# Mixer D of a hybrid encoder layer: heads computed in pairs, with scores on 64 rows of the array, the key bias added in the maximum's instruction, probabilities scaled before they are turned, and values as the stationary operand

## The reference

```python
c = jnp.cumsum(jax.nn.log_sigmoid(f_logit.astype(F32)), axis=1).transpose(0, 2, 1)
for blk in range(seq // D_QBLOCK):            # 8 blocks of 128 queries
    s = jnp.einsum('bhqd,bhkd->bhqk', qh[:, :, q0:q1], kh[:, :, :q1]) * HEAD_DIM ** -0.5
    s = s + c[:, :, q0:q1, None] - c[:, :, None, :q1]
    causal = jnp.arange(q1)[None, :] <= (q0 + jnp.arange(D_QBLOCK))[:, None]
    p = jax.nn.softmax(jnp.where(causal, s, -jnp.inf), axis=-1)
    outs.append(jnp.einsum('bhqk,bhkd->bhqd', p, vh[:, :, :q1]))
```

## Time and profile before

| | us |
|---|---|
| median of 3 runs | 2148.26 (2148.06 to 2148.79) |
| the profiled execution, its own time | 2147.65 |
| its span, first to last instruction | 2145.9 |
| first to last filler matmul of mixer D | 615.25 to 964.0 |
| TensorE idle in 615.25 to 964.50 | 0.57 |

### The profile page before, as it was taken

How to read it: one execution, slowest core, us unless ns; L and a number is a source line. 1 busy time by engine, 2 the same in 40 slices (tenths; PEclk the granted TensorE clock), 3 DMA queues, 4 the chain that set the end, 5 groups by cost and what they waited for, 6 DMA issues and landing times. The chain is left out here.

```text
span 2145.9 us, 23081 instructions
## 1 busy us (share of the span) xinstructions
PE 2065.3 (96%) x7129; PEld 1091.9 (51%) x7130; DVE 1073.3 (50%) x2957; ACT 430.1 (20%) x929; POOL 686.9 (32%) x605
## 2 busy tenths in 40 slices
PE   7999999999999999999999999899999999999992
PEld 5445887574644555554444554444444444444440
DVE  6121455549452222221224756786666666666645
ACT  2111332334321111112221222011111111111113
POOL 1752002212132221202442001355544555544531
PEclk9999999999999999999999999999999999999996
DMA  5421000011112121216336004699999999999984
GB/s 142 120 89 39 21 15 26 20 45 64 50 65 74 68 74 49 69 49 235 103 93 226 30 40 162 248 335 345 354 357 352 358 356 358 352 355 346 345 270 166
DMA packets 129901, 368.24 MB, mean 172 GB/s; under 512 B 34332, under 2 KB 66192, under 8 KB 104352
## 3 DMA queue, kind: packets, MB, share of 16 engines
q1 hardware_dynamic: 104224, 312.64, 38.9%
q0 software_dynamic: 23520, 54.61, 10.6%
q10 hardware_dynamic: 2080, 0.01, 0.1%
HBM read 318.37 MB, written 68.16 MB: 180 GB/s over the span
## 5 line engine op out<-in xcount | busy, mean ns | idle before, releaser
L2993 PE MATMUL banks<-arena 128*128 128x512 f32 x1056 | 470.5, 599 | 7.6 <-DVE arena L2986 3.5
L2972 POOL DMA_INDIRECT arena<-h_rows,index x268 | 276.6, 1032 | 151.0 <-issue 75.1
L2993 PEld LDWEIGHTS banks<-arena 128*128 128x128 f32 x1056 | 195.8, 190 | 232.0 <-issue 227.7
L1712 PE MATMUL banks<-arena 128*128 128x512 f32 x616 | 279.7, 595 | 0.4 <-ACT arena L329 0.4
L3009 PE MATMUL banks<-arena 128*128 128x512 f32 x528 | 237.6, 592 | 1.3 <-ACT arena L2808 0.8
L285 PE MATMUL banks<-arena 128*128 128x512 f32 x480 | 220.2, 596 | 3.3 <-PEq L108 3.0
L2986 DVE STREAM_TRANSPOSE arena<-arena 128x1024 f32<-128x1024 f32 x66 | 133.9, 2029 | 138.0 <-PE banks L2993 138.0
L2980 POOL DMA_INDIRECT sums<-arena,row_to x66 | 107.1, 1623 | 275.2 <-DMA sums<-arena,row_to 256.4
L1712 PEld LDWEIGHTS banks<-arena 128*128 128x128 f32 x616 | 110.5, 190 | 116.1 <-issue 115.1
L3009 PEld LDWEIGHTS banks<-arena 128*128 128x128 f32 x528 | 100.2, 190 | 127.0 <-issue 125.3
L2956 DVE TENSOR_SCALAR index<-row 32x1 uint32<-32x1 f32 x1072 | 155.5, 145 | 17.1
(11 more groups left out here) (397 smaller groups left out, 2361.3 us busy)
## 6 DMA issues: line engine op xcount, KB each, us to landing
arena<-in_w_exp_gate_dram SPq DMA_DIRECT2D x66, 1024.0 KB, 8.4
arena<-in_w_exp_up_dram SPq DMA_DIRECT2D x66, 1024.0 KB, 10.7
arena<-in_w_exp_down_dram SPq DMA_DIRECT2D x66, 1024.0 KB, 19.7
arena<-in_w_in_dram SPq DMA_DIRECT2D x26, 1024.0 KB, 5.2
gates<-arena SPq DMA_DIRECT2D x60, 256.0 KB, 2.0
arena<-gates SPq DMA_DIRECT2D x60, 256.0 KB, 2.6
arena<-h_rows,index POOLq DMA_INDIRECT x268, 7.9
arena<-in_x_dram SPq DMA_DIRECT2D x8, 512.0 KB, 6.3
```

The costliest lines, as they stand in the source:

```text
L1712: mm = pe.matmul(gate_bank(n, b), left[:, k, :], right[:, k, :], start=(alone and k == 0), stop=(k == 3), skip_group_check=True)
L2972: return pool.indirect_dma_start(w.x[k][:, 256 * q:256 * (q + 1)], None, rows, bass.IndirectOffsetOnAxis(ap=g.index[:, k, q:q + 1], axis=0 ...
L2993: mm = pe.matmul(g.bank[:, 2, :].rearrange("p (a f) -> p a f", a=2), xT[:, k, :], wgu[:, :, k, :], start=(k == 0), stop=(k == KT - 1))
```

## The change

Units become pairs of heads: 16 units `t`, `i, c = divmod(t, 2)`, in which `e` is 0 or 1 for the two heads of the pair `c`.

- The keys are stored once, both heads in 128 rows, with no zeros and no bias row. The scores of head `e` use the rows 64e to 64e+63 of queries and keys, so each matmul has 64 rows and lies on one half of the array, and the two heads' matmuls alternate. Head 0 writes banks 0 and 1, head 1 writes 2 and 3.
- The key bias is laid out over all 128 partitions: VectorE scales `g.rows` in place, SyncE writes four rows to DRAM (`drops`) and reads each pair back broadcast (`bias[0]`, `bias[1]`, 1 MB each). One VectorE instruction (`biased`) adds it to the scores, multiplies by 0.125, writes the result to SBUF (`probs[e]`) and takes the maximum.
- ScalarE's exponential now reads SBUF and writes in place. When both heads are done, VectorE takes the reciprocal of the sums, and ScalarE multiplies the probabilities by it, again in place.
- The turn handles both heads' tiles as one list.
- In `values` the values (128x64) are stationary and the turned probabilities (128x128) stream. Head `e` writes the partitions 64e to 64e+63 of bank 5, so the result stands already turned; the turn of the block and its wait are gone. ScalarE copies it out.
- Scores are no longer double buffered, and a unit is finished before the next begins: score(t), 4 parts, 4 parts, turn(t), the remaining parts, values(t). Before the last `values` stand all the parts that remain.
- GpSimd's copy and three fills before the first unit, and two fills in mixer B, are gone.

```diff
-    g.kD = region(R1 + 2048, 2, 2, T)
+    g.kD = region(R1 + 2048, 2, T)
...
-    slot(whole(DK), fm(halves(g.kD[:, 0], 0)) + fm(halves(g.kD[:, 1], 0), P))
+    slot(whole(DK), fm(plain(g.kD[:, 0, :])) + fm(plain(g.kD[:, 1, :]), P))
...
-        pool.memset(g.kD[HD:P, :, 0, :], 0.0).then_inc(zeroed, 1)
-        pool.memset(g.kD[0:HD, :, 1, :], 0.0).then_inc(zeroed, 1)
...
+    def rows_of(e):
+        return slice(e * HD, (e + 1) * HD)
...
     def sync(sp):
         sp.wait_ge(s["drop"], 1)
-        for h in range(4):
-            at = HD if h % 2 == 0 else 0
-            sp.dma_start(g.kD[at:at + 1, h // 2, h % 2, :], drop[4 + h:5 + h, :]).then_inc(drop_in, 16)
+        sp.dma_start(drops, g.rows[4:8]).then_inc(s["kept"], 16)
+        sp.wait_ge(s["kept"], 16)
+        for c in range(2):
+            if c:
+                sp.wait_ge(g.c_yT_read, NT)
+            sp.dma_start(bias[c], drops[2 * c:2 * c + 2].rearrange("(a e) n -> a e n", a=1).to_broadcast(
+                [P, 2, T])).then_inc(bias_in[c], 16)
...
-        pe.wait_ge(s["ones"], 2)
-        pe.wait_ge(drop_in, 64)
...
+        def score(t):
+            i, c = divmod(t, 2)
+            n = (i + 1) * P
+            if t:
+                pe.wait_ge(s["mx"], 2 * t)
+            for a in range(0, n, HALF):
+                z = min(n, a + HALF)
+                for e in range(2):
+                    pe.matmul(bank[:, 2 * e + a // HALF, 0:z - a], g.qD[rows_of(e), c, i * P:n],
+                              g.kD[rows_of(e), c, a:z], start=True, stop=True, skip_group_check=True)
+            for e in range(2):
+                pe.matmul(bank[:, 2 * e + i // 4, (i % 4) * P:(i % 4 + 1) * P], g.ident16[:], g.neg_above[:],
+                          start=False, stop=True, skip_group_check=True).then_inc(s["S"], 1)
...
+        def values(t):
+            i, c = divmod(t, 2)
+            pe.wait_ge(s["pTr"], first_turn[t + 1])
+            if t:
+                pe.wait_ge(s["yTr"], t)
             for kt in range(i + 1):
+                for e in range(2):
+                    h = 2 * c + e
+                    mm = pe.matmul(bank[rows_of(e), 5, 0:P], g.vD[:, kt, h * HD:(h + 1) * HD],
+                                   probsT[:, e * (i + 1) + kt, :], start=(kt == 0), stop=(kt == i),
+                                   skip_group_check=True)
...
+        for t in range(N):
+            left = len(parts) // (N - t)
+            score(t)
+            fill(4, ("score", t))
+            fill(4, ("weigh", t))
+            turn(t)
+            fill(max(left - 8 - 2 * (len(groups(t)) - 1), 2) if t + 1 < N else len(parts), ("values", t))
+            values(t)
...
+        def biased(t, e):
+            dve.wait_ge(s["S"], 2 * t + 1 + e)
...
+            dve.tensor_tensor_reduce(out=probs[e][:, 0:n], in0=flat[:, 0:n], in1=bias[c][:, e, 0:n], scale=0.125,
+                                     scalar=floor[:], op0=ALU.add, op1=ALU.max,
+                                     accum_out=mx[:, t, e:e + 1]).then_inc(s["mx"], 1)
...
+            for e in range(2):
+                act.wait_ge(s["neg"], 2 * t + 1 + e)
+                act.activation(probs[e][:, 0:n], probs[e][:, 0:n], ACT.Exp, bias=neg[:, t, e:e + 1],
+                               accum_out=den[:, t, e:e + 1]).then_inc(s["P"], 1)
+            copy(("score", t))
+            act.wait_ge(s["rd"], t + 1)
+            for e in range(2):
+                act.activation(probs[e][:, 0:n], probs[e][:, 0:n], ACT.Copy,
+                               scale=den[:, t, e:e + 1]).then_inc(s["sc"], 1)
+            copy(("values", t))
+            act.wait_ge(s["pv"], t + 1)
+            act.activation(g.yT[:, 8 + c, i * P:(i + 1) * P], bank[:, 5, 0:P], ACT.Copy).then_inc(s["yTr"], 1)
```

More of the change, by code:

```diff
@@ L1727, in tensor @@
         pe.wait_ge(g.c_yT_read, NT)
-        pe.wait_ge(s["ones"], 2)
-        pe.wait_ge(drop_in, 64)
[L1731 to L1759, removed]
-                mm.then_inc(s["pT"], 1)
@@ L1779, in tensor @@
[L1779 to L1785, removed]
-            if i >= 2:
-                values(i - 2)
-                if i > 2 and (i - 2) % 4 == 0:
-                    turn_y((i - 2) // 4 - 1)
-        turn_y(NT - 1)
-        fill(len(parts), "end")
+        def score(t):
[11 more added lines that the diff above has]
+                          start=False, stop=True, skip_group_check=True).then_inc(s["S"], 1)
@@ new lines, in turn @@
+        def turn(t):
+            n = t // 2 + 1
+            for k, tiles in enumerate(groups(t)):
+                if k:
+                    fill(2, ("turn", t, k))
+                if first_turn[t] + k:
+                    pe.wait_ge(s["pTr"], first_turn[t] + k)
+                pe.wait_ge(s["sc"], 2 * t + 1 + (tiles.stop > n))
+                for f in tiles:
+                    e, kt = divmod(f, n)
+                    mm = pe.transpose(bank[:, 4, (f % 4) * P:(f % 4 + 1) * P], probs[e][:, kt * P:(kt + 1) * P],
+                                      g.ident[:])
+                mm.then_inc(s["pT"], 1)
@@ L1799, in vector @@
         dve.tensor_tensor(t4, tok[1][0], t2, ALU.subtract).then_inc(s["tsum"], 1)
-        dve.wait_ge(g.c_yT_read, NT)
-        dve.tensor_scalar(drop, g.rows[:], -8.0, None, ALU.mult).then_inc(s["drop"], 1)
         joined = [0]
@@ new lines, in weigh, with turned @@
+        def weigh(t):
+            dve.wait_ge(s["P"], 2 * t + 2)
+            dve.reciprocal(den[:, t], den[:, t]).then_inc(s["rd"], 1)
+        def turned(t):
+            if t:
+                dve.wait_ge(s["pv"], t)
+            for k, tiles in enumerate(groups(t)):
+                if k:
+                    join(("turn", t, k))
+                dve.wait_ge(s["pT"], first_turn[t] + k + 1)
+                dve.tensor_copy(probsT[:, tiles.start:tiles.stop, :].rearrange("p a n -> p (a n)"),
+                                bank[:, 4, 0:len(tiles) * P]).then_inc(s["pTr"], 1)
@@ L1859, in scalar @@
+        join("start")
+        dve.wait_ge(s["drop"], 2)
+        for t in range(N):
+            if t < 2:
+                dve.wait_ge(bias_in[t], 16)
+            for e in range(2):
+                biased(t, e)
+            join(("score", t))
+            weigh(t)
+            join(("weigh", t))
+            turned(t)
+            join(("values", t))
     def scalar(act):
-        def read_yT(i):
-            act.wait_ge(s["yT"], i + 1)
-            act.activation(g.yT[:, 8:10, i * P:(i + 1) * P],
-                           bank[:, 4, 0:256].rearrange("p (c n) -> p c n", c=2), ACT.Copy).then_inc(s["yTr"], 1)
```

111 lines of the change are left out of this document (26 added, 85 removed).

## The result

The changed kernel takes 2122.1 us (median of the runs, 2120.6 to 2122.9; one far-off run of 3371 us at a granted clock of 0.597 is left out), against 2148.5 before (2148.06 to 2149.68). The ratio is 0.9869, with an interval of 0.9856 to 0.9882: 1.3% faster, 26.4 us, where 16 had been forecast. The profiled execution took 2121.3, with a span of 2119.6 against 2145.9.

What follows compares the result with a forecast made beforehand. TensorE's own matmul starts were taken to bound mixer D. Gains of 9.9 (scores), 10 (values), 2.3 (block turns) and 1.8 (end) less 8.0 (switches) made 16.0 us less, 2132 us; range 2124 to 2152.5.

Steps and rivals of the forecast that it cites:

- Scores: Score matmuls of mixer D: two heads on two row halves overlap in part, 31.0 to 21.1 us, gain 9.9.
- three slots for four records: Score matmuls: with starts in order and one record per half at a time, a pair's four records take three slots.
- Values: Value matmuls of mixer D: overlap on two column halves, gain taken as 10 us, between 0 and 13.8.
- the caution on the loads: Value matmuls: four 64-column loads at 0.054 fill two slots of 0.108 exactly, so 10 us was taken instead of 13.8.
- C: Rival on scores and values: full overlap, 15.5 us each, 2121 us in all; chance 8%.
- rival B: Rival on the values: row halves overlap, column halves don't, so 6 us less, 2142 us; chance 15%.
- Switches: Changes of the array shape in use, three in each of 16 units: 0.50 us a unit, 8.0 us lost.
- The chain: From masks to turn at 1024 keys: data ready after 6.4 us, just covered by eight filler parts; counted 0.
- Rival D: Rival on the bias instruction: twice as long a column, so turns wait 7.6 us in all, 2140 us; chance 10%.
- The start: Start of mixer D: removed copies lay beside filler, the bias may come 3 us after the scores; worth 0.
- The end: End of mixer D: last values and copy fit in the 2.6 us the spill needs behind the filler; gain 1.8.
- rival A: Rival on scores and values: nothing overlaps, switches are all loss, 3.7 us slower, 2152 us; chance 20%.

## Why the forecast missed

**The stage's arithmetic held.** TensorE's starts alone set the length of the stage; no other engine became the bound.

**Scores: 15.5, not 9.9.** This step failed: "If starts stay in order and each half is busy with one record at a time", then "three slots for four records". A record that waits for its half does not hold up the other half, up to about four records ahead, so four records take two slots. The starts leave the program's order, as the values by whole heads show; whether one queue is searched or each half keeps a few records in wait, they don't tell. Per pair of heads 2n columns stream one behind the other, 15.5 us in all; putting both heads on one half gave back 15.7.

**Values: 15.5, not 10.** The same step failed, "by the same counting" (1.7 us), and so did the caution on the loads. It had 64 columns at 0.054 a load and two halves "exactly full"; it was exactly full and cost nothing: 32 loads in 1.73 us, 0.054 each, beside records that start in pairs every 0.108. One half gave back 14.1, of the 13.8 that lie within the stretch. By its own counting of slots the forecast had 13.8 here; the other 3.8 went for that caution. It gave this case (C) 8% because "the order of the records is against it". The trace of before had no pair on two halves, so that order was an assumption and should have stood as an even choice between two prices, not as an argument.

The Trainium skill, TensorE: Matmul & The Clock Gate, Part 3, lets a weight load run beside a matmul only when the row groups differ. The values' loads cover all 128 rows, as their matmuls do, and run beside them: 1.73 us of PEld within 1.97 of PE. By that rule alone rival B would have come true; the measurement decides. The same part of the page has matmuls start strictly in the program's order; the values by whole heads disagree, in their starts and in their 28 slots, where strict order gives 31. TensorEngine Tiling (Array Packing), Tiling Modes, which makes a change of mode cost a drain, is borne out by the added seams, 0.20 us each.

**Switches: 7.4, not 8.0.** Read from the unit above, each seam as the delay up to the next line's first start: filler to values 0.09 (914.63 was due, 914.72 came; forecast 0.15), values to scores 0.17 (1.90 over 16 x 0.108; 0.20), scores to mask 0.20 (1.92 over 4 x 0.43; 0.15; half of it is the first pair of scores, which takes 0.53 instead of 0.43), mask to filler nothing. That is 0.46 a unit where 0.50 was forecast, 7.4 in all, of which 0.3 at the last unit lie behind the stretch. From the stretch: 15.5 of scores, 2.3 of block turns, and 17.3 of values (31.1 less the 13.8 still in it) make 35.1; 29.3 were measured, so 5.8, 1.3 less than the seams' 7.1. Those 1.3 are a term that the forecast's sum of the stage had too small: the scores of before took 32.2 in the stretch, not the 31.0 of their columns, because in 24 of the 32 groups the first record takes 0.05 us longer than those behind it. The change made this 1.3 go too. It is also half of the 2.5 by which the stage before lay above its sum.

**Block turns: 2.3, right.** **The chain: right.** Timeline with 1024 keys:

```profile
896.39 0.28 PE L1734 MATMUL banks<-neg_above,ident 128*128 128x128 bf16 x2
896.65 1.28 DVE L1805 CUSTOM_DVE_ANT_0 arena<-banks,arena,floorD 128x1024 f32<-128x1024 f32 x1 [4.78 <-PE banks L1734]
...
898.17 1.15 ACT L1859 ACTIVATE arena<-arena,negD 128x1024 f32<-128x1024 f32 x1 [3.31 <-DVE negD L1809]
899.62 1.15 ACT L1859 ACTIVATE arena<-arena,negD 128x1024 f32<-128x1024 f32 x1 [0.20 <-DVE negD L1809]
900.76 0.57 ACT L1850 ACTIVATE arena<-banks 128x512 f32<-128x512 f32 x1
901.24 2.18 ACT L1864 ACTIVATE arena<-arena,denD 128x1024 f32<-128x1024 f32 x2
...
903.43 0.60 PE L1747 MATMUL banks<-ident,arena 128*128 128x128 f32 x4
```

The bias with the maximum takes 1.28 (forecast 1.29). The two scalings take 2.18, so head 0 is ready near 902.3, 5.9 after the mask where 6.4 was forecast, and the turn starts 7.0 after it without a wait. Rival D is out. Eight parts are about what this chain needs; five are too few.

**The start: right.** The broadcasts of the bias are issued at 626.2 and 626.6 and land 4.6 and 7.2 us later. The first is there at 630.8, when the first scores only start (630.84), so nothing waits for it: VectorE takes a filler product until 631.63 and begins with the bias at 631.67. The second is there at 633.8, long before its pair's turn.

**The end: 0.7, not 1.8.** The last values do stand in the idle time behind the filler, but the merge starts 4.24 after the filler's end instead of 3.16. (The 2.0 that rival A's sum takes for the end is not worked out anywhere; nothing hangs on it.)

```profile
936.88 1.97 PE L1759 MATMUL banks<-arena 128*64 128x128 f32 x32
...
937.61 0.32 SPq L1654 DMA_DIRECT2D gates<-arena  x1
938.89 0.28 ACT L1868 ACTIVATE arena<-banks 128x128 f32<-128x128 f32 x1 [1.31 <-PE banks L1759]
...
941.07 7.51 PE L285 MATMUL banks<-arena 128*128 128x512 f32 x13 [2.23 <-PEq L108]
```

The step that failed is that the values and their copy "fit in the 2.6 that the spill needs". The spill does not need 2.6: no one waits for it to land, and in the kernel before SyncE was through with issuing it at 965.55, 1.1 us behind the filler's end. That was the last thing ahead of the barrier. Now the last thing is ScalarE's copy of the last values, done at 939.17, 2.4 us behind the filler's end, so 1.3 of the time of values and copy stand in the open. In the waits of SyncE at the end of the block (times, longest) 0.2 has become 1.3, before and then after:

```profile
SPq L811 <- PEq L811: 0.2, 1, 0.2
```

```profile
SPq L811 <- PEq L811: 1.3, 1, 1.3
```

What follows that barrier is of one length in both kernels: the first matmul of the merge comes 2.0 us behind the spill's issue before, and 1.9 behind the copy now. It is no wait for data. `release` (L104 to L108) has GpSimd clear the semaphores and then holds a second barrier for all engines, where SyncE waits 1.4 us before and 1.3 after:

```profile
SPq L108 <- PEq L108: 1.4, 1, 1.4
```

```profile
SPq L108 <- PEq L108: 1.3, 1, 1.3
```

The values by whole heads bear this out: their last unit is 1.36 longer, and the merge stands 6.04 behind the start of the last filler record instead of 4.7.

**The sum.** 15.5 of scores and the 1.3 that they had cost above their columns, 15.5 of values, 2.3 of block turns and 0.7 at the end, less 7.4 of switches, are 27.9 less. The spans differ by 26.3, with the stage's later start (0.75), its 0.7 of wait and 0.2 behind the mixer in them: 27.9 without. The size missed by the two overlap terms, 11.1 together; the others by 1.3 at most.

## What to carry to other kernels

Where float32 matmuls use 64 rows or give 64 columns, put two independent ones on the two halves within four records of each other: they then cost as much as one, whatever their order within those four. Count about 0.2 us for each change of shape that drains the array, 0.1 where little is to load, and keep two halves' work together so that there are few. Where neither end of a cost is in the trace, don't let a model of the order make one of them unlikely.

No kernel measured here is faster than the changed one; values in runs of two and scores by head come out the same. Pairing the other mixers' products in the same way was not tried.

## What the runs showed of the hardware

- Two float32 records on different row halves, or on different column halves, start together and cost one: 0.43 us a pair of 512 columns, 0.108 a pair of 128.
- A half works ahead of the program's order, by about four records: runs of one head of up to 4 records cost 0 to 0.5 us over the stage, runs of 8 cost 5.1, whole heads 8.4.
- Weight loads of 64 columns in float32 go at 0.054 us each beside matmuls over all rows.
- A change of shape shows as 0.76 us of idle before the weight load, yet costs 0.09 to 0.20; that idle figure is not a loss.
- The first record behind a change of line or of head holds the array, or its half, longer than the ones that follow: 0.05 us in the scores of before and in the values, 0.10 in the scores on 64 rows.
- From the last work in a stage's block to the next stage's first matmul are 1.9 to 2.0 us here, spent on two barriers and the clearing of semaphores. The last values and their copy stand ahead of it and are not hidden.
- Open: how the array comes to take records up to four ahead, and whether that is a count of records or of matmuls.
